# Split buffers of its own for the last retention head, its sums of squares started late and shared with ScalarE, and the forget-gate arithmetic moved behind an eviction

## What is computed

```python
def rmsnorm(x, g):
    y = x * lax.rsqrt(jnp.mean(x * x, axis=-1, keepdims=True) + EPS) * g

# layer 0
h = h + 0.5 * swiglu_ffn(h, ffn1)
h = h + retention_mixer(rmsnorm(h, mix_g))      # 4 heads; ends in o @ w_out
h = h + 0.5 * swiglu_ffn(h, ffn2)               # starts with rmsnorm(h, ffn2_g)
k, v, fl = split(rmsnorm(h, kv_g) @ w_kvf)      # shared keys, values, gate inputs
logf = log_sigmoid(fl + b_f)                    # cumulated over the tokens
# layer 1: swiglu, forgetting attention over k, v, cumsum(logf), swiglu, final rmsnorm
```

## Time and profile before

| what | us |
|---|---|
| median of three runs | 2589.04 (2588.89 to 2590.99) |
| the profiled execution | 2587.03 |
| its span, first to last instruction | 2584.9 |
| TensorE busy in the span | 2547.3 |
| VectorE busy | 1038.9 |
| ScalarE busy | 680.7 |
| GpSimd busy | 347.2 |

### The profile page before, as it was taken

The page is one execution under the profiler, slowest core; times in us unless marked ns, Lnnn a source line. Parts: engine busy times, 40 slices in busy tenths (PEclk is TensorE's granted clock), DMA queues, the critical chain, the costliest instruction groups (busy, mean ns, idle before and its releaser), DMA issues.

```text
span 2584.9 us, 43818 instructions
## 1 busy us (share of the span) xinstructions
PE 2547.3 (99%) x18707; PEld 2448.6 (95%) x18707; DVE 1038.9 (40%) x1516; ACT 680.7 (26%) x950; POOL 347.2 (13%) x273
## 2 busy tenths in 40 slices
PE   9999999999999999999999999999999999999998
PEld 8999999979797978999999999999998789999998
DVE  4332334453444455332334343332335754332333
ACT  4221222121212222221222232212223542221221
POOL 0100113120101103100113221100121022100112
PEclk9999999999999999999999999999999999999999
DMA  5232332222222213232332442322323432232231
GB/s 149 81 102 62 90 95 81 82 70 74 80 67 83 61 53 90 81 100 64 89 94 71 135 116 82 93 78 74 92 86 96 119 86 75 84 100 68 82 96 47
DMA packets 393652, 221.70 MB, mean 86 GB/s; under 512 B 8032, under 2 KB 385984, under 8 KB 393520
## 3 DMA queue, kind: packets, MB, share of 16 engines
q1 hardware_dynamic: 388688, 205.13, 27.5%
q0 software_dynamic: 4640, 14.58, 1.7%
q10 hardware_dynamic: 192, 0.04, 0.0%
HBM read 206.01 MB, written 13.71 MB: 85 GB/s over the span
## 4 chain that ended last, share of the span: by engine, by line
PE 96%; DVE 2%; ACT 1%; issue 0%; DMA 0%; SPq 0%; POOL 0%; ACTq 0%; DVEq 0%; POOLq 0%
PE ps L1458 87%; PE ps L1644 1%; PE ps L1700 1%; PE ps L1829 1%; PE ps L1636 1%; DVE wl L562 1%; PE ps L1857 1%; PE ps L1881 1%; PE ps L1654 0%; DVE xl L861 0%; PE ps L1734 0%; PE ps L1620 0%; DVE h L906 0%; DMA xtok<-in_x_sample 0%; PE ps L1693 0%
## 5 line engine op out<-in xcount | busy, mean ns | idle before, releaser
L562 DVE TENSOR_TENSOR wl<-raw,wh 128x1024 fp32r<-128x1024 f32 (+3 forms) x352 | 450.9, 1281 | 1297.3 <-ACT wh L557 1297.3
L1458 PE MATMUL ps<-xh,wl 128*128 128x288 f32 x4000 | 862.8, 297 | 5.9 <-DVE xl L861 2.7
L1458 PE MATMUL ps<-xl,wh 128*128 128x288 f32 x4000 | 853.3, 295 | 0.0
L1458 PE MATMUL ps<-xh,wh 128*128 128x288 f32 x4000 | 853.1, 295 | 0.0
L557 ACT CAST wh<-raw 128x1024 fp32r<-128x1024 f32 (+3 forms) x352 | 375.6, 1067 | 1173.6 <-PE ps L1458 1172.6
L1458 PEld LDWEIGHTS ps<-xh,wl 128*128 128x128 f32 x4000 | 642.1, 189 | 14.6 <-issue 7.2
L1458 PEld LDWEIGHTS ps<-xl,wh 128*128 128x128 f32 x4000 | 643.0, 189 | 0.0
L1458 PEld LDWEIGHTS ps<-xh,wh 128*128 128x128 f32 x4000 | 643.0, 189 | 0.0
L1458 PE MATMUL ps<-actl,wh 128*128 128x288 f32 x1408 | 300.7, 294 | 0.0
L1458 PE MATMUL ps<-acth,wl 128*128 128x288 f32 x1408 | 300.7, 295 | 0.0
L1355 POOL TENSOR_TENSOR rsilu<-silu,rstd 128x576 f32<-128x576 f32 x88 | 125.8, 1430 | 1295.5 <-ACT silu L610 1295.5
(11 more groups left out here) (230 smaller groups left out, 1586.2 us busy)
## 6 DMA issues: line engine op xcount, KB each, us to landing
raw<-in_ffn_w_in SPq DMA_DIRECT2D x176, 512.0 KB, 3.8
raw<-in_ffn_w_out SPq DMA_DIRECT2D x32, 768.0 KB, 4.8
raw<-in_ret_w_in SPq DMA_DIRECT2D x48, 512.0 KB, 3.8
raw<-in_ffn_w_out SPq DMA_DIRECT2D x32, 640.0 KB, 4.4
raw<-in_ret_w_out SPq DMA_DIRECT2D x32, 256.0 KB, 2.7
raw<-in_fox_w_kvf SPq DMA_DIRECT2D x16, 512.0 KB, 4.0
raw<-in_fox_w_q SPq DMA_DIRECT2D x8, 512.0 KB, 5.1
bias<-cum_scratch SPq DMA_DIRECT2D x16, 256.0 KB, 3.3
```

The costliest lines, as they stand in the source:

```text
L562: nc.vector.tensor_tensor(wl[:, s % SPLIT, 0:kt, :], raw[:, s, 0:kt, :], wh[:, s % SPLIT, 0:kt, :].bitcast(F32), ALU.subtract).then_inc(lo ...
L1458: mm = nc.tensor.matmul(out[:, a:z], w, x[:, a:z], start=start and n == 0, stop=stop and n == len(terms) - 1)
```

## The change

It has five parts.

1. Head 3 gets split buffers of its own, `ogh2` (over `qk`, read out by then) and `ogl2` (over `rt`). ScalarE splits the first two gated tiles at once and only then does the weight cast of the filler unit, and VectorE forms the first two low parts before the filler's `wl` and `h`. Output units of head 3 read the new buffers. A wait of TensorE before the first turned tile (for the first new state) is taken out, in all heads.
2. GpSimd starts the sums of squares when output unit 4 is taken (`SQUARES_AT`), not unit by unit. It squares tiles 0 to 3; ScalarE squares tiles 4 to 7 into `hsq`, each behind the `xh` of that tile, and GpSimd only adds those.
3. `ffn2_0` takes the order of `ffn1_0`: sums of the partitions behind unit 1, spread in unit 2, and both engines split weights for unit 3 before the first eviction.
4. In `v`, `take_gates` (the two copies from PSUM) stays before the first eviction; the rest of `log_gates` comes behind it.
5. The stores of the gates and of their sums go to SyncE, behind the loads for `v` and ahead of those for `ffn1_1`.

```diff
+SQUARES_AT = 4
...
+        place["ret_last"] = place["ret"]
         qk = sb("ret", "qk", [P, 4, T])
+        ogh2 = sb("ret_last", "ogh2", [P, 4, T], F32R)
...
+        place["ret_last"] = place["ret"]
         ogh = sb("ret", "ogh", [P, 4, T], F32R)
+        hsq = sb("ret_last", "hsq", [P, KD // 2, T])
...
+        place["ret_last"] = place["ret"]
         rt = sb("ret", "rt", [P, 6, T])
+        ogl2 = sb("ret_last", "ogl2", [P, 4, T], F32R)
...
             plain(tiles_of(A["fox_w_kvf"][:, D:2 * D]), "v")
+            sp.wait_ge(ftok_ready, 1)
+            sp.dma_start(O["logf_prompt"][0].rearrange("(i p) h -> p i h", p=P), ftok[:, 0:4, :]).then_inc(f_stored, 16)
+            sp.dma_start(O["logf_sample"][0], ftok[0:TS, 4, :]).then_inc(f_stored, 16)
+            sp.wait_ge(cum_ready, 1)
+            sp.dma_start(cum_dram, cumf[:, :]).then_inc(cum_stored, 16)
...
                 ahead(beside(hd, 6))
-                ahead(beside(hd, 7))
+                if hd < HEADS - 1:
+                    ahead(beside(hd, 7))
+                    act.wait_ge(unit_done, beside(hd, 7) + 1)
                 for f in range(4):
+                    if hd == HEADS - 1 and f == 2:
+                        ahead(beside(hd, 7))
 
                     act.wait_ge(ogt_ready, 8 * hd + 2 * f + 2)
-                    act.wait_ge(unit_done, beside(hd, 7) + 1)
-                    nc.scalar.copy(ogh[:, f, :], ogt[:, f, :]).then_inc(ogh_ready, 1)
+                    nc.scalar.copy((ogh if hd < HEADS - 1 else ogh2)[:, f, :], ogt[:, f, :]).then_inc(ogh_ready, 1)
...
                 x_tile(n, G_FFN2)
+                if n >= KD // 2:
+                    nc.scalar.activation(hsq[:, n - KD // 2, :], h[:, n, :], ACT.Square).then_inc(hsq_ready, 1)
             act.wait_ge(sp_stored, 16 * HEADS)
-            ffn("ffn2_0", G_KV)
+            ffn("ffn2_0", G_KV, ahead=lambda: None)
...
+                def low_parts(f0, f1):
+                    hi, lo = (ogh, ogl) if hd < HEADS - 1 else (ogh2, ogl2)
+                    for f in range(f0, f1):
+                        dve.wait_ge(ogh_ready, 4 * hd + f + 1)
+                        nc.vector.tensor_tensor(lo[:, f, :], ogt[:, f, :], hi[:, f, :].bitcast(F32), ALU.subtract) \
+                            .then_inc(og_ready, 1)
                 gated(0)
                 gated(1)
+                if hd == HEADS - 1:
+                    low_parts(0, 2)
                 advance(beside(hd, 7))
                 gated(2)
                 gated(3)
...
+                low_parts(2 if hd == HEADS - 1 else 0, 4)
...
-            ffn("ffn2_0", G_KV, make_rstd)
+            ffn("ffn2_0", G_KV, lambda: take_rstd(6), lambda: token_rstd(6))
...
-            def log_gates():
+            def take_gates():
 
                 dve.wait_ge(zt_done, 1)
...
+
+            def log_gates():
...
                     if n == KD:
-                        log_gates()
+                        take_gates()
...
                     nc.vector.tensor_tensor(kvt[:, s % 2, :], unit_psum(s), rstd[:, :], ALU.mult) \
                         .then_inc(taken, 1)
+                    if n == KD:
+                        log_gates()
...
                 for j in range(tiles):
...
+                    square = sq[:, :]
+                    if j < squared:
+                        ready(j)
+                        out = sq if j else ssq
+                        nc.gpsimd.tensor_tensor(out[:, :], h[:, j, :], h[:, j, :], ALU.mult).then_inc(sq_step, 1)
+                        n_sq[0] += 1
+                        pool.wait_ge(sq_step, n_sq[0])
+                    else:
+                        pool.wait_ge(hsq_ready, j - squared + 1)
+                        square = hsq[:, j - squared, :]
                     if j:
-                        add = nc.gpsimd.tensor_tensor(ssq[:, :], ssq[:, :], sq[:, :], ALU.add)
+                        add = nc.gpsimd.tensor_tensor(ssq[:, :], ssq[:, :], square, ALU.add)
...
-            sum_squares(h_taken(RET_O[HEADS - 1]))
+            pool.wait_ge(taken, RET_O[HEADS - 1] + SQUARES_AT + 1)
+            sum_squares(h_taken(RET_O[HEADS - 1]), squared=KD // 2)
...
-                        late = u0 == 0
+                        late = u0 in (0, first["ffn2_0_in0"])
...
-                        if waits is not None and norm and s == 0 and not late:
-                            sum_partitions()
+                        if waits is not None and norm and s == late and u0:
+                            sum_partitions(6 if late else 4)
...
-                pe.wait_ge(sn_ready, 2 * hd + 1)
                 turned(0)
```

More of the change, by code:

```diff
@@ L312, in encoder @@
         ssx_ready = sem("ssx_ready")
+        hsq_ready = sem("hsq_ready")
         xhi_ready = sem("xhi_ready")
@@ L1110, in head @@
                 gated(3)
-                for f in range(4):
-                    dve.wait_ge(ogh_ready, 4 * hd + f + 1)
-                    nc.vector.tensor_tensor(ogl[:, f, :], ogt[:, f, :], ogh[:, f, :].bitcast(F32), ALU.subtract) \
-                        .then_inc(og_ready, 1)
+                low_parts(2 if hd == HEADS - 1 else 0, 4)
             nc.vector.memset(mv[:, :, :], 1.0).then_inc(setup, 1)
@@ L1322, in _, with sum_squares @@
             n_sq, n_norm, n_pair = [0], [1], [0]
-            def sum_squares(ready, tiles=KD):
+            def sum_squares(ready, tiles=KD, squared=KD):
                 if n_norm[0] > 1:
@@ L1602, in output @@
                     last = hd == HEADS - 1
-                    unit(u, u % 4, 4, ogh, ogl, (lambda k: pe.wait_ge(og_ready, 4 * hd + k + 1)) if n == 0 else None,
+                    unit(u, u % 4, 4, ogh2 if last else ogh, ogl2 if last else ogl, (lambda k: pe.wait_ge(og_ready, 4 * hd + k + 1)) if n == 0 else None,
                          DEEP if last else 2, 2 if last and n < 2 else None)
```

10 lines of the change are left out of this document (removed).

## The result

The changed kernel takes 2576.36 us (median of five runs, 2572.71 to 2578.5) against 2589.04 us before (five runs, 2588.87 to 2590.99): a ratio of 0.9949, 95% interval 0.9934 to 0.9963, that is 12.7 us less. The prediction was 2577.8 us in a range of 2573.8 to 2583.2, faster at 0.93. The profiled execution is the quickest of the five, 2572.71 us with a span of 2571.0, where the profiled one of before had 2587.03 and 2584.9.

What follows compares the result with a forecast made beforehand. TensorE, busy 2547.3 of 2584.9 us, bounds the kernel, so only its idle or half-speed time can go. Parts 1 to 3 net 7.5, gates 2.2, stores 1.5: 11.2 us less, median 2577.8 us, range 2573.8 to 2583.2.

Steps and rivals of the forecast that it cites:

- a stall of 1.5 us instead of 3.2: Head 3, unit 0: with own split buffers TensorE runs blocks 0 and 1 early, then waits 1.5 us, not 3.2.
- The removed wait for the state: Before the first turned tile: worth 0 to 1 us at most, counted as 0 because the second state's wait follows.
- About 3 us for the last `xl`: First unit of `ffn2_0`: after 7 blocks TensorE waits about 3 us for VectorE's last `xl`, ready at 988.8.
- the blocking: Head 3's output units: two-input VectorE and GpSimd instructions wait for each other's whole instruction; late rounds take about 5.3 us.
- The reading by mere sharing of bandwidth: Same stretch: if VectorE and GpSimd only shared bandwidth, it ends about 1 us earlier and the sum is 12.2 us.
- The 9.1 us of parts 1 to 3: Through the first three units of `ffn2_0`: finished at 1004.5 instead of 1013.6, 9.1 us earlier before any clock loss.
- The charge: Behind the 3 us stall for the last `xl`: TensorE's lower clock costs 1.6 us, between 0 and about 5.
- The case with the milder clock: Rival for 953 to 1005 us: milder blocking or no clock loss, gain 13 to 14 us, 2575.5 us; chance 0.16.
- the sluggish VectorE: Rival: the last `xl` comes no earlier than before, at 993.5; gain 5.5 us, 2583.5 us; chance 0.06.
- the other store: Rival at `ffn1_1`: the last store of `v` lands late, the 1.5 us wait stays, 2579.3 us; chance 0.05.
- the slow clock all through: Rival, also called "slower", 953 to 1005 us: TensorE stays at the low level, 20 us more, 2596 us; chance 0.02.
- The dearer clock: Rival for stalls within 35 us: low clock costs about 5 us, gain 7.8 us, 2581.2 us; chance 0.14.

Runs made afterwards that it cites:

- The late eviction: Changed kernel with VectorE's eviction of head 2's last unit moved behind head 3's four low parts: 2573.84 us, ratio 0.9945; also run with all squares on ScalarE: 2569.54 us.
- The second profile of the changed kernel: The changed kernel run again, unaltered, beside three variants on the same chip: median 2575.36 us, ratio 0.9953 to the kernel before.
- the whole share: Changed kernel with all eight squares on ScalarE; GpSimd only adds, four of seven additions after the last `xl`: 2570.13 us, ratio 0.9931 to before.

## Why the prediction was right

**Part 1.** The step was a stall of 1.5 us instead of 3.2, inside unit 0 and ahead of block 2: it is 1.32, there. Unit 0 was to end at 956.4; its last twelve matmuls start at 955.43 and those of unit 1 at 957.16, 956.5 without the late first stage. The shorter stall was to leave the clock alone: it did in every profile that has it. The removed wait for the state was counted at 0: the wait of 0.99 us before the first turned tile is gone, and one of 0.77 us stands behind that tile, for the second state, the cover that the prediction named. No run has this wait back alone. The late eviction shows what half of the stall in unit 0 was: 0.66 of the 1.31.

**Part 2.** Units 1 to 7 without a wait for `wl`: so it is. The wait of 1.5 before `ffn2_0`: 1.52. About 3 us for the last `xl`: 3.02. GpSimd from 971 to 990: 972.2 to 991.15, the same with 0.7 us of a later start. The last `xl` was to be ready at 988.8; it ends at 989.87, 989.2 without that 0.7. Durations under contention fit the blocking: 0.69 us for a 512-wide `wl` with GpSimd silent, 2.44 for a 1024-wide one beside it, 1.23 without. The Trainium skill, "SBUF — State Buffer", section "Who interferes with whom", states this exclusion, and the trace agrees. The reading by mere sharing of bandwidth would have made the sum 12.2 instead of 11.2 us and so come nearer to the 12.7 measured, but for a wrong reason: the waits of 1.52 and 3.02 us are those of the blocking. The 1.4 us that the medians have beyond the forecast may be clock or spread; no run shows which. ScalarE's squares take 0.67 us, where I had 0.8, bring no table load and delay nothing on ScalarE's side, as charged.

What the prediction did not see is that half of part 2 is idle. It costed ScalarE's share only for harm on ScalarE. Without the share the waits are the same or shorter, since GpSimd's queue in units 5 to 7 is full with or without it, and with it of the longer additions. Nor did it see that part 2 by itself (2.1 us of the stage) can be lost again to the clock: the times show no gain from it. The 9.1 us of parts 1 to 3 came out as a sum; their split was not forecast.

**Part 3.** Sums of 1.2 us behind the second unit, `ssq` early: 1.15 us, and `ssq` stands 6 us ahead of it (991.15 to 997.22). The gain of parts 1 to 3 without the clock was put at 9.1 us and measured at 8.85. The late sums by themselves, though, are worth nothing that the times show while part 2 is there. Before, the clock fell at the sums, behind only 1.65 us of idleness, and so it did in the kernel with parts 4 and 5 alone; where part 2 is undone and the sums come one unit later, it did not fall behind the same 1.67 us. That the sparse sums right behind the wait make the difference is argued from these three profiles, not shown: no run changed it alone with several profiles.

**The clock.** The charge was 1.6 us. Eight profiles have a stall of 2.5 to 3.0 us before the last `xl` (the changed kernel twice, and six of its variants). They lost 0, 1.7 (five times) and 3.4 us (twice). Four other profiles, whose longest wait there is 1.04 to 1.67 us, lost nothing; the two of kernels without parts 1 to 3 lost 3.4 us behind waits of 1.65 and 1.66 us, with the sums right behind. So the size of the charge is what is seen most often, but the reasoning behind it, that the same stall brings the same loss, is not borne out: the loss differs between executions of one kernel, and that the median came so close to the forecast is partly luck. This and a fall in attention are also where most of the 6.7 us between two profiles of one and the same kernel comes from: 2579.4 against 2572.71 us. The second profile of the changed kernel has

```profile
990.00:995.00 5.00, 4.11 (x17) 4.12 (x18) 1.95 (x2) 1.05 (x1) 2.02 (x2) 0.50 0.17 51
995.00:1000.00 5.00, 5.00 (x34) 5.00 (x33) 0.11 (x1) 0.00 (x0) 0.00 (x0) 0.83 0.38 108
...
1970.00:1975.00 5.00, 3.15 (x23) 2.61 (x24) 3.74 (x16) 3.96 (x14) 0.00 (x0) 0.80 0.01 3
1975.00:1980.00 5.00, 5.00 (x42) 4.88 (x39) 2.95 (x7) 2.77 (x7) 0.00 (x0) 0.86 0.57 160
```

that is 3.4 us of clock at the stall, of which 2.6 lengthen the stage (the rest falls into the wait), and 1.7 in attention, which cost 1.5. Its first stage is 1.0 us longer (unit 0 at 956.39 instead of 955.43), and behind the last sums it takes 1.1 us more. Together these are, within 0.1 us, the 6.1 us between the spans.

**Parts 4 and 5.** 2.2 predicted, 2.3 measured; 1.5 predicted, 1.7 measured. The edit that undoes part 5 alone brings 1.8 us back in that stage. SyncE's first load for `ffn1_1` goes out at 1497.39; the earlier trace rows moved by the 10.4 us of that stage would be 1494.1, so it is 3.3 us late where 2.5 was said, and nobody waits for it.

**The sum.** 9.1 + 2.2 + 1.5 = 12.8 without the clock against 8.85 + 2.3 + 1.7 = 12.85 by the landmarks. The forecast of 2577.8 us is 1.4 over the median, less than the spread between runs. The case with the milder clock (2575.5) is the one that the profiled execution shows in its rows; the median lies between it and the forecast. The two profiled executions lie 14.3 us apart, a little more than in either case; 1.5 us of it are the fall of the clock in attention in the one of before; so the step from profile to median, which was taken as 2.0 us, is 3.65 for the changed kernel. The rivals of the sluggish VectorE, the other store and the slow clock all through did not come about: no wait for `ssq`, none near 1540, and never more than 3.4 us of clock lost in that stretch in a profile of this kernel. The dearer clock was not far, though: the second profile has twice the charge. The price of the "slower" rival holds for 45 us spent at the low level (0.44 of them are 20); 45 us of work at half speed would take 45 us more.

## What to carry to other kernels

When two engines exclude each other on a port, count the instructions of the less urgent one that fall *before the last one of the urgent one*. Total work saved there is worth nothing if what is saved would have run afterwards, and a third engine that can do the squares in its idle time is worth most when it empties exactly that stretch. Here half a share changed no wait for the better, and the whole share, with four additions held back, took 3.1 us of waits.

Several waits of about 1 us and one wait of 3 us with a smaller sum can cost the same, since behind the long one TensorE's clock may fall. Compare waits in one profile, but judge the clock over several executions, and compare stage by stage: the start of the same instruction in two traces keeps a fall of the clock elsewhere out of the account.

## What was not expected of the hardware

Two executions of one kernel, with the same three waits to 0.01 us, differ by 6.7 us, and 4.1 of them are two places where the granted clock fell in one of them. The loss is not spread: in this stretch it was 0, 1.7 or 3.4 us. A wait of 1.3 us left the clock at its higher level in all nine profiles that have it, and the stall of 3.2 us before unit 0 was followed by a mean of 0.66 to 0.69 over 955 to 960 us in all three that have that one.

ScalarE's square of 128x576 elements takes 0.67 us and GpSimd's 1.14. ScalarE's does not lengthen VectorE's work beside it: `xl` is 0.82 us with and without a square on ScalarE at the same time.
